# Encoder trunk on one core: the activation tiles spaced by 1088 bytes instead of 1024

## The reference, cut to what matters

```python
for i in range(DEPTH):                       # DEPTH = 2
    x = x + 0.5 * swiglu(rmsnorm(x, norm_ff1[i]), ff1_w_gate[i], ff1_w_up[i], ff1_w_down[i])
    x = x + token_mixer(rmsnorm(x, norm_mix[i]), w_in[i], ...)
    x = x + 0.5 * swiglu(rmsnorm(x, norm_ff2[i]), ff2_w_gate[i], ff2_w_up[i], ff2_w_down[i])
    g = jax.nn.sigmoid(rmsnorm(x, norm_ple[i]) @ ple_w_gate[i])
    x = x + g * (p[i] @ ple_w_proj[i])
return rmsnorm(x, norm_final)

def swiglu(h, w_gate, w_up, w_down):         # d_ff = 2816
    return (jax.nn.silu(h @ w_gate) * (h @ w_up)) @ w_down
```

## Time and profile before

| | us |
|---|---|
| median of 3 runs | 1306.4 (1305.42 to 1307.3) |
| the profiled execution, its own time | 1306.64 |
| its span, first to last instruction | 1304.7 |
| busy in the span: TensorE matmuls | 1265.1 (97%) |
| TensorE weight loads (beside the matmuls) | 1168.5 (90%) |
| VectorE | 738.4 (57%) |
| ScalarE | 588.8 (45%) |
| GpSimd | 92.7 (7%) |

### The profile page before, as it was taken

One profiled execution on the slowest core, in us unless ns is written; L12 is line 12 of the kernel. 1 busy time (PEld: TensorE's weight loads), 2 busy tenths in 40 slices (PEclk: granted clock), 3 DMA queues, 4 the chain that ended last, 5 costly groups with the idle time before them and its releaser, 6 DMA issues.

```text
span 1304.7 us, 21474 instructions
## 1 busy us (share of the span) xinstructions
PE 1265.1 (97%) x8836; PEld 1168.5 (90%) x8836; DVE 738.4 (57%) x766; ACT 588.8 (45%) x671; POOL 92.7 (7%) x120
## 2 busy tenths in 40 slices
PE   6999999999999999999999999999999999999996
PEld 6999997999989899999789999889898989999985
DVE  4554445577657554554665444557686565454464
ACT  5433434555544543334544344446455354433453
POOL 0000001001420100000000000000034100000000
PEclk9999999999999999999999999999999999999999
DMA  6656564455325365555536556654543355555541
GB/s 244 197 190 193 192 209 152 156 164 162 130 98 186 129 226 179 177 190 201 186 128 209 181 192 193 194 164 135 187 130 129 100 184 165 192 191 193 194 176 50
DMA packets 162562, 223.36 MB, mean 171 GB/s; under 512 B 10400, under 2 KB 134208, under 8 KB 162496
## 3 DMA queue, kind: packets, MB, share of 16 engines
q1 hardware_dynamic: 162496, 222.41, 52.1%
HBM read 221.35 MB, written 1.05 MB: 170 GB/s over the span
## 4 chain that ended last, share of the span: by engine, by line
PE 93%; DVE 2%; ACT 1%; POOL 1%; issue 1%; DMA 1%; SPq 0%; POOLq 0%; DVEq 0%; ACTq 0%
PE bank L375 29%; PE bank L376 29%; PE bank L377 29%; PE bank L654 2%; PE bank L431 1%; PE bank L635 1%; PE bank L540 1%; DMA raw<-in_ff_w_up 1%; POOL mean L1111 1%; DVE xn L1182 1%; PE bank L680 1%; PE bank L684 0%; DVE x L1507 0%; ACT xn L824 0%; PE bank L620 0%
## 5 line engine op out<-in xcount | busy, mean ns | idle before, releaser
L1171 DVE TENSOR_TENSOR w_lo<-raw,w_hi 128x2048 fp32r<-128x2048 f32 x204 | 471.2, 2310 | 362.4 <-ACT w_hi L812 362.3
L375 PE MATMUL bank<-h_hi,w_hi 128*128 128x256 f32 x1824 | 518.4, 284 | 2.3 <-ACT relu L890 2.3
L377 PE MATMUL bank<-h_lo,w_hi 128*128 128x256 f32 x1824 | 516.3, 283 | 0.0
L376 PE MATMUL bank<-h_hi,w_lo 128*128 128x256 f32 x1824 | 516.3, 283 | 0.0
L812 ACT ACTIVATE w_hi<-raw 128x2048 fp32r<-128x2048 f32 x204 | 389.1, 1907 | 145.9 <-PE bank L377 143.2
L375 PEld LDWEIGHTS bank<-h_hi,w_hi 128*128 128x128 f32 x1824 | 349.9, 192 | 7.5 <-issue 5.7
L376 PEld LDWEIGHTS bank<-h_hi,w_lo 128*128 128x128 f32 x1824 | 350.0, 192 | 1.5
L377 PEld LDWEIGHTS bank<-h_lo,w_hi 128*128 128x128 f32 x1824 | 349.9, 192 | 0.0
L375 PE MATMUL bank<-w_hi,small_hi 128*128 128x512 f32 x368 | 144.4, 392 | 0.0
L376 PE MATMUL bank<-w_hi,small_lo 128*128 128x512 f32 x368 | 143.7, 390 | 0.0
L377 PE MATMUL bank<-w_lo,small_hi 128*128 128x512 f32 x368 | 143.2, 389 | 0.0
(11 more groups left out here) (135 smaller groups left out, 996.5 us busy)
## 6 DMA issues: line engine op xcount, KB each, us to landing
raw<-in_ff_w_gate SPq DMA_DIRECT2D x44, 1024.0 KB, 5.2
raw<-in_ff_w_up SPq DMA_DIRECT2D x44, 1024.0 KB, 5.2
raw<-in_ff_w_down SPq DMA_DIRECT2D x44, 1024.0 KB, 4.9
raw<-in_w_in SPq DMA_DIRECT2D x44, 1024.0 KB, 5.0
raw<-in_w_out SPq DMA_DIRECT2D x8, 1024.0 KB, 4.9
raw<-in_ple_w_gate SPq DMA_DIRECT2D x8, 1024.0 KB, 4.9
raw<-in_w_branch_a SPq DMA_DIRECT2D x4, 1024.0 KB, 4.9
raw<-in_w_branch_b SPq DMA_DIRECT2D x4, 1024.0 KB, 5.0
```

The costliest lines, as they stand in the source:

```text
L375: pe.matmul(o, lh, rh, start=start, stop=False)
L376: pe.matmul(o, ll, rh, start=False, stop=False)
L377: return pe.matmul(o, lh, rl, start=False, stop=stop)
L1171: dve.tensor_tensor(w_lo[:, s, :], raw[:, s, :], w_hi[:, s, :].bitcast(F32), ALU.subtract).then_inc(lo_ready[s], 1)
```

## The change

The rows of `h_hi` and `h_lo` get 16 elements more at the end of each tile, which nothing reads or writes. A tile starts 1088 bytes behind the one before instead of 1024. The views that the rest of the kernel uses have the same shape as before.

```diff
 SLOTS = 3
+SKEW = 16
 TURNS = CHUNKS // SLOTS
@@
-        h_hi = sb("h_hi", [P, 8, T], F32R)
-        h_lo = sb("h_lo", [P, 8, T], F32R)
+        h_hi, h_lo = (sb(name, [P, 8, T + SKEW], F32R)[:, :, 0:T] for name in ("h_hi", "h_lo"))
```

## The result

The changed kernel takes 1300.35 us (median of 7 runs, 1295.86 to 1302.56) against 1306.12 us (7 runs, 1304.96 to 1307.3). The ratio is 0.995, with a 95% interval of 0.9935 to 0.9966. The profiled execution took 1302.56 us with a span of 1300.8 us, 3.9 us less than before.

The account below looks back on a forecast made before the run. The prediction took TensorE's matmul steps to bound the kernel, 5472 of them at a rigid 0.120 us. All four terms, (a) to (d), were taken as 0, so it forecast an unchanged 1306.4 us, range 1304 to 1309 us.

Parts of the forecast that it names:

- The bound: Whole kernel: TensorE limits it, busy 1265.1 of 1304.7 us; 5472 matmuls streaming h take 0.120 us each, 657 us.
- (a): Elementwise instructions that write or read h: longer distance between blocks costs 0, at most 0.3 us either way.
- (b): Moving read of h tiles: one 512-byte boundary more or less costs 0, at most 1.7 us.
- (c): Moving read against weight load in the 5472 matmuls streaming h: 0, bounds 60 us down and 43 us up.
- the prediction's own sign: By-columns matmul steps: the prediction would be wrong if they differed from 0.120 us by over half a nanosecond.
- nearest row: Line 635 loading v: even and odd heads, offsets 0 and 256, take 1.09 and 1.08 us; hence 0.
- The bounds: Matmuls streaming h: at most 5472 x 11 ns = 60 us down, 4788 x 9 ns = 43 us up.
- (d): The 1056 matmuls with h as stationary operand: 0, bounds 12 us down and 10 us up.
- a part of the price: Half of the faster rival's chance of 0.16: only part of the 11 ns is clash, 1290 to 1303.8 us.
- Faster: Matmuls streaming h: loads clash now at equal starts modulo 512; skew frees seven tiles of eight, 53 us, 1254 us; chance 0.16.
- Slower: By-columns products: equal starts are quiet, seven tiles of eight leave them, up to 43 us more, 1349 us; chance 0.18.
- The third rival: Memory placing: 512 bytes may be no size the memory knows; time stays 1306.4 us; within the 0.66 for same.

Follow-up runs that it names:

- The map: Kernels without the model, timing float32r matmul steps with moving or stationary tiles at other places; 256 columns: 0.1133 to 0.1200 us a step; no kernel time.
- 64-byte: Against the kernel before the change: tiles stay 1024 bytes apart, h_hi and h_lo begin 64 bytes later; 1294.87 us, ratio 0.9909.
- 448-byte: Against the kernel before the change: tiles stay 1024 bytes apart, h_hi and h_lo begin 448 bytes later; 1287.73 us, ratio 0.9862.
- 32-byte: Against the kernel before the change: h_hi and h_lo begin 32 bytes later, with eight elements ahead and 120 behind; 1291.36 us, ratio 0.9889.

## Why the prediction was wrong

**The bound** held. TensorE's steps set the time, and all that moved was steps.

**(a) and (b)** held. Blocks in the elementwise work cost nothing (689 and 598 ns, against 689 and 597). Boundaries cost nothing by themselves: with both tiles moved together by 64 to 384 bytes they fall elsewhere in the moving tile, and the step stays 0.1200 us.

**(c) is the step that failed.** It put the term for moving read against weight load at 0, where the runs show -1.6 ns on each of 5472 matmuls, 8.5 us. By the prediction's own sign, half a nanosecond from 0.120 us, this is a miss of the mechanism and not of a size. The 0 had two grounds.

The first was that moving read and weight load pass through every distance once in each matmul, so that the start can't matter. The map shows that it does: 0.1200 us at distance 0, 0.1167 at 32 bytes, 0.1133 or 0.1178 at 448, with nothing else changed in the block. So an argument that lets every distance come by once and therefore sets the start aside doesn't hold. Nor is the start distance all, as the two steady steps for one distance show. That the two reads shift in time against one another is a guess: in the records a load begins 2 to 5 ns behind a matmul's start at either step, so they don't decide it.

The second ground was a wrong nearest row. The attention products of the earlier trace rows are plain float32 with 128 columns and step at 0.109 us; they don't show what float32r matmuls pay, and so could not show that a place costs them nothing. The same goes for the transposes of the earlier trace rows. The row that deserved doubt was the even 0.120 us of the earlier trace rows. I read it as rigid against every placing, but in the kernel before every tile has one and the same distance. The trace held no second placing of this form, and sameness in it was no evidence. The bounds, 60 us down and 43 us up, were right; 0 deserved less weight than 0.66.

**(d)** failed in sign of its own: h stationary isn't neutral but loses, 4.3 ns on each of 672 matmuls with 512 columns (the 384 with 256 columns gain 1.5 ns each). The change shifts one operand for both uses, and 512 columns want the distance that 256 columns don't.

**The rivals.** The time fell into the case of a part of the price, faster, between 1290 and 1303.8 us, which had a chance of 0.08. "Faster" had the place and the sign, and its ceiling of 11 ns is sound (the best settled step found is 6.7 ns below). Its mechanism was wrong in its terms: not seven tiles freed and one left, since tile 0 gained 6 ns over its three steps, like tile 4, and not a clash at equal starts modulo 512, since 256 bytes are like 0. "Slower" described the 512-column matmuls well, 2 to 7 ns dearer off distances 0 and 256, and had the wrong form for it. The third rival was right that 512 bytes is not the size that counts, but 256 is, and the time wasn't the same.

**The sum as it should have been**: 5472 steps x 1.56 ns = 8.5 us gained; 672 x 4.3 ns = 2.9 us lost; 1104 x 0.6 ns = 0.6 us lost: 5 us, which gives 1301 us. 1300.35 was measured. These sizes are read from the changed kernel's own trace, so the sum accounts for the result and doesn't test it; the experiments do that.

**The scatter.** The runs of the changed kernel spread over 6.7 us, those of before over 2.3. They follow the granted clock: 1295.86 us at 0.998, 1302.56 us at 0.991. At one clock, 0.994, three runs of the changed kernel took 1299.74 to 1300.59 us, and the profiled run before took 1306.64 us. In the profiled execution it fell to about half, the 1.2 GHz level, in four stretches of the changed kernel (columns as in the earlier trace rows). The longest lies where one layer passes to the next; between 640 and 660 us TensorE stood idle for 1.3 us, waiting for `xn`, and once for 3.0 us, waiting for nothing that the profile shows:

```profile
433.80:437.20 3.40, 3.40 (x18) 3.40 (x18) 1.16 (x2) 0.60 (x1) 0.00 (x0) 0.53 0.67 270
652.20:659.00 6.80, 5.61 (x26) 5.62 (x27) 5.36 (x6) 3.13 (x5) 2.94 (x3) 0.52 0.23 54
850.20:853.60 3.40, 3.40 (x12) 2.71 (x13) 1.19 (x2) 0.60 (x1) 0.00 (x0) 0.53 0.68 239
1075.50:1078.90 3.40, 3.40 (x19) 3.40 (x19) 1.10 (x2) 0.60 (x1) 0.00 (x0) 0.53 0.68 281
```

That is 17.0 us at half clock. In the longest the matmuls that hold h stationary, with 256 columns, step like this:

```profile
656.11 0.41 PE L375 MATMUL bank<-w_hi,h_hi 128*128 128x256 f32 x1
...
658.67 0.41 PE L375 MATMUL bank<-w_hi,h_hi 128*128 128x256 f32 x1
```

12 steps take 2.56 us, 0.2133 us each. That is 256 cycles of 1.2 GHz with nothing on top, and it is 0.213 us at half clock before the change and in the 64-byte, 448-byte and 32-byte kernels too. The 7 to 13 ns beyond the columns, and with them the effect of the distance, were seen only at full clock. The same view of the kernel before has three stretches, 10.2 us:

```profile
211.50:214.90 3.40, 3.28 (x10) 2.78 (x11) 1.42 (x3) 0.60 (x1) 0.00 (x0) 0.50 0.80 276
853.20:856.60 3.40, 3.40 (x12) 2.71 (x11) 0.69 (x1) 0.76 (x2) 0.00 (x0) 0.50 0.55 194
1078.50:1081.90 3.40, 3.40 (x19) 3.40 (x18) 0.89 (x2) 0.80 (x2) 0.00 (x0) 0.50 0.61 249
```

TensorE has no matmul in the half-clock stretch that ends either trace. The 6.8 us more cost up to 3.4 us, so the profiled pair (3.9 us apart) understates what the steps give. Why this kernel's clock varies more wasn't tested.

**What stays open** is what inside the chip makes the distance count. The runs show a period of 256 bytes, an effect of as little as 16 bytes, two steady steps for one distance (64 and 448 bytes), opposite preferences for 256 and 512 columns, and none of it at half clock. None shows the mechanism, nor all that decides between the two steps.

## What to carry to other kernels

Where float32r matmuls with a weight load each set the time, the place of the moving tile relative to the stationary one, modulo 256 bytes, is a free parameter, and a constant shift (32, 64 or 448 bytes here) is worth more than a skew, which mixes good and bad distances. Choose it for each form by itself, by the step from start to start on a small map of blocks, and let the map enter each block as the kernel does, since what runs before helps to pick the steady step. And an even row proves nothing about a parameter that the kernel never varies: ask first whether the trace holds a second value of it.

## What the runs showed of the hardware

- The settled step of a 128 x 128 by 256-column float32r matmul takes values from 0.1133 to 0.1200 us by placement and by what ran before, and that of 512 columns from 0.2267 to 0.2333 us, with all other engines idle. At half clock the 256-column step was 0.213 us with h stationary, before the change as well as with h at 32, 64 or 448 bytes.
- Of the two ports, the Trainium skill ("SBUF — State Buffer", section "Who interferes with whom") says that TensorE's two reads are independent and that it never waits on anyone. It doesn't wait on other engines here: the kernels' 0.1200 and 0.1183 us are the steps of the map, where these are idle. But where its own two operands lie relative to one another changes the step by up to 6.7 ns of 120; whether the two reads are what meets isn't shown.
- The Trainium skill ("TensorE: Matmul & The Clock Gate", section "Wait — 56ns, not 53.3ns?") gives a warm step of N / 2.4 GHz plus about 2.5 ns, N being the moving columns. It wasn't reached with float32r at any of the distances tried. The best was 113.3 ns for 256 columns, 6.7 ns above 256 cycles, and at distance 0 both lengths had 13.3 ns above theirs.
